# A mixture of experts on one core: the router product by token, the down matrices by column halves, and the first gather chunk by chunk

## The reference

```python
def expert_choice_moe(h, w_router, w_gate_e, w_up_e, w_down_e):
    b, s, _ = h.shape
    cap = EC_CAPACITY * s // N_EXPERTS                       # 64 tokens for each of 16 experts
    affinity = jax.nn.softmax((h @ w_router).astype(jnp.float32), axis=-1)
    top_aff, idx = lax.top_k(jnp.swapaxes(affinity, 1, 2), cap)
    bidx = jnp.arange(b)[:, None, None]
    xe = h[bidx, idx]
    hid = jax.nn.silu(jnp.einsum('becd,edf->becf', xe, w_gate_e)) * jnp.einsum('becd,edf->becf', xe, w_up_e)
    ye = jnp.einsum('becf,efd->becd', hid, w_down_e)
    return jnp.zeros_like(h).at[bidx, idx].add(ye * top_aff[..., None].astype(ye.dtype))

# in second_block, for each of the two layers i
x = x + expert_choice_moe(rms_norm(x, g_moe[i]), w_router[i], w_exp_gate[i], w_exp_up[i], w_exp_down[i])
```

## Time and profile before

| | |
|---|---|
| median of 3 runs | 3707.64 us (3706.45 to 3708.91) |
| the profiled execution: device time | 3712.06 us |
| its span | 3710.3 us |
| mean granted TensorE clock | 0.964 of full |
| TensorE matmul busy | 3504.9 us (94%) |
| weight loads busy | 2375.7 us (64%) |
| VectorE (DVE) busy | 1728.1 us (47%) |
| ScalarE (ACT) busy | 1142.2 us (31%) |
| bytes moved | 618.76 MB, mean 167 GB/s |

### The profile page before, as it was taken

The page is one execution under the profiler, slowest core; times in us unless marked ns, Lnnn a source line. Parts: engine busy times, 40 slices in busy tenths (PEclk is TensorE's granted clock), DMA queues, the critical chain, the costliest instruction groups (busy, mean ns, idle before and its releaser), DMA issues. The chain is left out here.

```text
span 3710.3 us, 44635 instructions
## 1 busy us (share of the span) xinstructions
PE 3504.9 (94%) x16784; PEld 2375.7 (64%) x16784; DVE 1728.1 (47%) x2908; ACT 1142.2 (31%) x1792; POOL 41.5 (1%) x20
## 2 busy tenths in 40 slices
PE   8899999979999999989998999999988997999997
PEld 6678877855788886747875434437746885444336
DVE  6665545378665538565334111137656334111116
ACT  5632223147422224365322000013355322000003
POOL 0000000022000000000000000000000000000000
PEclk9999999989999999989998999999989998999998
DMA  4223323120133231211225999971211324999991
GB/s 151 88 91 96 96 91 96 51 93 2 69 96 96 96 96 50 87 41 66 94 84 229 414 422 422 422 322 60 86 60 40 99 71 171 400 421 422 422 400 57
DMA packets 113080, 618.76 MB, mean 167 GB/s; under 512 B 12780, under 2 KB 13300, under 8 KB 63544
## 3 DMA queue, kind: packets, MB, share of 16 engines
q1 hardware_dynamic: 112952, 617.04, 44.0%
HBM read 614.81 MB, written 4.28 MB: 167 GB/s over the span
## 5 line engine op out<-in xcount | busy, mean ns | idle before, releaser
L398 PE MATMUL PS<-WK_r,RING_r 128*128 128x512 f32 x1920 | 749.6, 390 | 0.0
L396 PE MATMUL PS<-WK_r 128*128 128x512 f32 x1448 | 566.3, 391 | 0.0
L398 PEld LDWEIGHTS PS<-WK_r,RING_r 128*128 128x128 f32 x1920 | 360.3, 188 | 77.7
L390 ACT ACTIVATE WK_r<-RING 128x1024 fp32r<-128x1024 f32 x212 | 223.4, 1054 | 450.3 <-PE PS L398 369.8
L397 PE MATMUL PS<-HT_r,WK_r 128*128 128x512 f32 (+1 forms) x896 | 349.5, 390 | 0.0
L393 DVE TENSOR_TENSOR RING_r<-RING,WK_r 128x1024 fp32r<-128x1024 f32 x212 | 259.1, 1222 | 185.2 <-ACT WK_r L390 185.1
L396 PEld LDWEIGHTS PS<-WK_r 128*128 128x128 f32 x1448 | 271.7, 188 | 57.4 <-issue 0.5
L397 PE MATMUL PS<-HT_r,RING_r 128*128 128x512 f32 (+1 forms) x752 | 295.9, 393 | 0.0
L2479 PE MATMUL PS<-AR,WK 128*64 128x512 f32 x1152 | 264.0, 598 | 0.0
L398 PE MATMUL PS<-AR_r,RING_r 128*128 128x512 f32 x672 | 262.6, 391 | 0.0
L393 DVE TENSOR_TENSOR RING_r<-RING,RING_r 128x1280 fp32r<-128x1280 f32 (+2 forms) x96 | 132.5, 1381 | 274.2 <-ACT RING_r L390 274.2
(11 more groups left out here) (450 smaller groups left out, 5296.0 us busy)
## 6 DMA issues: line engine op xcount, KB each, us to landing
AR<-moe SPq DMA_DIRECT2D x192, 1024.0 KB, 13.4
RING<-moe SPq DMA_DIRECT2D x160, 1024.0 KB, 13.6
RING<-ff_in SPq DMA_DIRECT2D x96, 512.0 KB, 3.5
RING<-branch SPq DMA_DIRECT2D x64, 640.0 KB, 3.9
WK<-moe SPq DMA_DIRECT2D x32, 1024.0 KB, 13.9
RING<-ff_out SPq DMA_DIRECT2D x48, 512.0 KB, 3.5
RING<-mix_in SPq DMA_DIRECT2D x44, 512.0 KB, 3.6
RING<-ple SPq DMA_DIRECT2D x16, 640.0 KB, 5.4
```

What stands on the lines that cost most here:

```text
L390: return nc.scalar.activation(r(out), x, ACT.Copy)
L396: nc.tensor.matmul(out, r(w_high), r(x_high), start=start, stop=False)
L398: return nc.tensor.matmul(out, r(w_low), r(x_high), start=False, stop=stop)
```

## The change

Three things are changed in both layers.

1. `route`: the router's weights are loaded in the stage before (`load_router`, issued by SP in `out_stage` behind the prefetch of its weights). The product is turned round: the tokens of `HT` are the stationary operand and the 16 columns of `WR` move, 4 token tiles for each of the 8 chunks, which writes the logits with tokens on partitions at once. ACT's copy and the transposes of L2355 go. DVE adds the squares in pairs only, and TensorE sums the four pairs (4 by 4 matmuls with one moving column). ACT loads the root's table ahead of its wait for the mean.
2. `experts`, down matrices: the data of the 8 pieces are laid out anew by the host, so that the first four hold the left 512 output columns of all eight chunks and the last four the right ones (`down_step`). ACT and DVE take each half when its four steps are done. In the last pair the back steps 0 to 3 stand behind the down steps 4 to 7, and the back steps 4 to 7 write banks 0 to 3 without a wait for DVE's adds.
3. `experts`, first pair: `first_tokens(k)` gathers one chunk; two stand ahead of the first matrix step, and one behind each of the steps 0 to 5. ACT copies chunk by chunk.

```diff
+    router_in = whole.enter_context(nc.semaphore("router_in"))
+    WR = SM[:, 128:128 + KD * EXPERTS]
+    def load_router(l):
+        return lambda sp: sp.dma_start(WR, io["router"][l]).then_inc(router_in, 16)
...
             def _(sp):
-                sp.dma_start(WR, io["router"][l]).then_inc(s["w_in"], 16)
                 for j in range(MOE_R):
...
             def _(pe):
-                pe.wait_ge(s["w_in"], 16)
+                pe.wait_ge(router_in, 16 * (l + 1))
                 for k in range(KD):
                     pe.wait_ge(s["scaled"], k + 1)
-                    mm = nc.tensor.matmul(bank(0)[0:EXPERTS], WR[:, k * EXPERTS:(k + 1) * EXPERTS], HT[:, k],
-                                          start=(k == 0), stop=(k == KD - 1))
+                    for t in range(TT):
+                        mm = nc.tensor.matmul(bank(1, t * EXPERTS, EXPERTS), HT[:, k, t * P:(t + 1) * P],
+                                              WR[:, k * EXPERTS:(k + 1) * EXPERTS], start=(k == 0 and t == 0),
+                                              stop=(k == KD - 1), skip_group_check=True)
                 mm.then_inc(s["logits_in"], 1)
-                pe.wait_ge(s["paired"], 6)
-                for t in range(TT):
-                    for k in (0, 4):
-                        mm = nc.tensor.matmul(bank(7, t, 1), SQ[k][:, t * P:(t + 1) * P], cst("ones", 0, 1),
-                                              start=(k == 0), stop=(k == 4))
+                for n in range(KD // 2):
+                    pe.wait_ge(s["paired"], n + 1)
+                    for t in range(TT):
+                        mm = nc.tensor.matmul(bank(7, t, 1), SQ[2 * n][:, t * P:(t + 1) * P], cst("ones", 0, 1),
+                                              start=(n == 0 and t == 0), stop=(n == KD // 2 - 1), skip_group_check=True)
                 mm.then_inc(s["summed"], 1)
-                pe.wait_ge(s["logits_out"], 1)
-                for t in range(TT):
-                    mm = nc.tensor.transpose(bank(1, t * EXPERTS, EXPERTS), LT[:, t * P:(t + 1) * P],
-                                             cst("ident")[0:EXPERTS, 0:EXPERTS])
-                mm.then_inc(s["logits_t"], 1)
...
-                act.wait_ge(s["logits_in"], 1)
-                nc.scalar.activation(LT, bank(0)[0:EXPERTS], ACT.Copy).then_inc(s["logits_out"], 1)
+                nc.scalar.preload_act_table(ACT.Sqrt)
...
+                def down_step(i, n):
+                    q = 2 * KD + n
+                    pe.wait_ge(moe_filled[q % MOE_R], before + i * (16 * UN // MOE_R) + 16 * (q // MOE_R + 1))
+                    w = moe_slot(q)
+                    half = n // 4
+                    for row in range(2):
+                        k = 2 * (n % 4) + row
+                        for e in range(2):
+                            mm = nc.tensor.matmul(bank(4 + half)[e * CAP:(e + 1) * CAP], HI[:, k, e * CAP:(e + 1) * CAP],
+                                                  w[:, (2 * row + e) * TOK:(2 * row + e + 1) * TOK],
+                                                  start=(k == 0), stop=(k == KD - 1))
+                    mm.then_inc(s["used"], 1)
...
-                    if k >= 2:
+                    b = k - 4 if final and k >= 4 else 6 + k % 2
+                    if k >= 2 and b >= 6:
                         pe.wait_ge(s["added"], i * KD + (k - 1))
...
-                    for k in range(KD):
-                        matrix_step(i, 2 * KD, 4, HI, k)
-                        if k == 1:
+                    for n in range(KD):
+                        down_step(i, n)
+                        if n == 1:
                             select(parity)
+                        if final and n >= 4:
+                            back_step(i, n - 4, True)
...
-                for k in range(KD):
-                    back_step(PAIRS - 1, k)
+                for k in range(4, KD):
+                    back_step(PAIRS - 1, k, True)
...
-                    act.wait_ge(s["used"], i * UN + UN)
                     act.wait_ge(s["sel_out"], i * 3 + 3)
-                    nc.scalar.activation(r(YH), PS[:, 4:6], ACT.Copy, scale=VALUE).then_inc(s["y_high"], 1)
+                    for half in range(2):
+                        act.wait_ge(s["used"], i * UN + (2 * KD + 4 + 4 * half))
+                        nc.scalar.activation(r(YH[:, half]), bank(4 + half), ACT.Copy, scale=VALUE).then_inc(s["y_high"], 1)
...
-                y_low(PAIRS - 1)
-                add_back(PAIRS - 1)
+                y_low(PAIRS - 1, (0,))
+                add_back(PAIRS - 1, range(4))
+                y_low(PAIRS - 1, (1,))
+                add_back(PAIRS - 1, range(4, KD), True)
```

More of the change, by code:

```diff
@@ L2320, in route @@
     def route(l, pw):
-        WR = SM[:, 128:128 + KD * EXPERTS]
         AF = AFID[:, :, 1:EXPERTS + 1]
@@ L2324, in route @@
         SQ = [wk(k) for k in range(KD)]
-        LT, AT, PL = (wk(16 + n)[0:EXPERTS] for n in range(3))
+        AT, PL = (wk(17 + n)[0:EXPERTS] for n in range(2))
         VALS = wk(19)[0:EXPERTS, 0:CAP]
         logits = lambda: bank(1, 0, TT * EXPERTS).rearrange("p (t e) -> p t e", t=TT)
-        with stage("w_in scaled squared paired logits_in logits_out logits_t summed mean root act_exp aff_ready aff_t tok_t tok_out "
+        with stage("scaled squared paired logits_in summed mean root act_exp aff_ready aff_t tok_t tok_out "
                    "picked places_t hots dve_step") as (block, s):
@@ L2399, in _ @@
                     v.tensor_scalar(HT[:, k], XT[:, k], par("moe_g", l * KD + k), None, ALU.mult).then_inc(s["scaled"], 1)
-                defer_sums(dve, s, SQ)
+                for k in range(0, KD, 2):
+                    dve.wait_ge(s["squared"], k + 2)
+                    v.tensor_tensor(SQ[k], SQ[k], SQ[k + 1], ALU.add).then_inc(s["paired"], 1)
                 dve.wait_ge(s["summed"], 1)
                 v.tensor_scalar(R4, bank(7, 0, TT), 1.0 / D, EPS, ALU.mult, ALU.add).then_inc(s["mean"], 1)
-                dve.wait_ge(s["logits_t"], 1)
+                dve.wait_ge(s["logits_in"], 1)
                 step(v.tensor_reduce(MX, logits(), X, ALU.max, negate=True))
@@ L2462, in token_step, with first_tokens @@
                         mm.then_inc(s["x_in"], 1)
[L2464 to L2469, removed]
+                def first_tokens(k):
+                    for t in range(TT):
+                        mm = nc.tensor.matmul(bank(4 + k % 4, k // 4 * P, P), HN[:, t, k * P:(k + 1) * P],
+                                              HOTS[0][:, t], start=(t == 0), stop=(t == TT - 1))
                     mm.then_inc(s["first_in"], 1)
@@ L2504, in pair @@
                     if first:
-                        for n in range(2):
-                            first_tokens(n)
+                        first_tokens(0)
+                        first_tokens(1)
                     else:
@@ L2509, in pair @@
                     for k in range(KD):
-                        if first and k % 2 == 0:
-                            pe.wait_ge(s["first_out"], k // 2 + 1)
+                        if first:
+                            pe.wait_ge(s["first_out"], k + 1)
                         matrix_step(i, 0, 0, XE[parity], k)
-                        if first and k in (1, 3):
-                            first_tokens(2 + k // 2)
+                        if first and k + 2 < KD:
+                            first_tokens(k + 2)
                         if not first and k >= 2:
@@ L2564, in pair @@
                         taken(i + 1, 1 - parity)
-                    act.wait_ge(s["used"], i * UN + UN)
                     act.wait_ge(s["sel_out"], i * 3 + 3)
-                    nc.scalar.activation(r(YH), PS[:, 4:6], ACT.Copy, scale=VALUE).then_inc(s["y_high"], 1)
[L2569 to L2572, removed]
+                    for half in range(2):
+                        act.wait_ge(s["used"], i * UN + (2 * KD + 4 + 4 * half))
+                        nc.scalar.activation(r(YH[:, half]), bank(4 + half), ACT.Copy, scale=VALUE).then_inc(s["y_high"], 1)
+                for k in range(KD):
+                    act.wait_ge(s["first_in"], k + 1)
+                    nc.scalar.activation(XE[0][:, k], bank(4 + k % 4, k // 4 * P, P), ACT.Copy).then_inc(s["first_out"], 1)
                 pair(0, 0)
@@ L2581, in _, with y_low, add_back @@
                 v = nc.vector
-                def y_low(i):
-                    dve.wait_ge(s["y_high"], i + 1)
-                    for half in range(2):
+                def y_low(i, halves=(0, 1)):
+                    for half in halves:
+                        dve.wait_ge(s["y_high"], i * 2 + (half + 1))
                         v.scalar_tensor_tensor(r(YL[:, half]), bank(4 + half), VALUE, r(YH[:, half]).bitcast(F32), ALU.mult,
                                                ALU.subtract).then_inc(s["y_low"], 1)
-                def add_back(i):
-                    for k in range(KD):
+                def add_back(i, ks=range(KD), spread=False):
```

(7 more changed lines are left out.)

9 lines of the change are left out of this document (4 added, 5 removed).

## The result

| | before | after |
|---|---|---|
| median of 7 runs each | 3707.64 us | 3721.99 us (3719.25 to 3725.17) |
| ratio, 95% interval | | 1.0037 (1.0027 to 1.0047) |
| profiled execution; its span | 3712.06; 3710.3 us | 3722.43; 3720.7 us |
| mean granted TensorE clock | 0.964 | 0.962 |
| TensorE matmuls busy | 3504.9 us | 3518.2 us |

The account below looks back on a forecast made before the run. TensorE was taken to set the pace in the experts' loop, and route to be a chain. Terms 14.0 + 2.6 - 2.4 = +14.2 us, set on the 3707.64 us median, gave 3721.8 us, 0.38% slower; range 3713 to 3729.

Parts of the forecast that it names:

- Part 1, route: Route: load wait removed, but 96 narrow records mostly at half clock; +14.0 us for two layers, bounds +10.8 to +17.2.
- The wait's end: Route: TensorE starts its product at about 1974.45 instead of 1975.77, no longer waiting for the router's weights.
- the 17 records at the full clock: Route: 17 records at 0.115 us fit before the clock falls at 1976.43; the other 79 take 0.215 each.
- the 7.0 forecast: Route: the mean starts at 1993.4 instead of 1986.42, +7.0 us a layer.
- bounds of 5.4 to 8.6: Route, mean's delay a layer: +5.4 with full clock for twice as long, +8.6 with low clock from the start.
- Rival 1: Route: the clock comes back in the new product as in the old; +1.0 us a layer, total 3709.8; chance 0.15.
- A gain of 1.3 us: Route: what removing TensorE's wait for the load of the router's weights saves in a layer.
- Rival 3: Whole kernel faster: needs 7.4 us, while the load's wait and the tail give at most 5.8; chance 0.03.
- Part 2, gather: Experts' first pair: four more gather places at 0.33 us, +1.3 us a layer; two layers +2.6, bounds 0 to +8.6.
- rival 2: First gather keeps the clock low longer and the tail gains little: +19.0 us, 3726.6; chance 0.10.
- Part 3, the tail: Down matrices and last pair's end: -1.2 us a layer; two layers -2.4, bounds -3.2 to -1.0.
- smaller gain: End of experts: if the adds keep the old pace of 0.92 us, they end at 2490.5, a gain of 0.5.

Follow-up runs that it names:

- e_route: The kernel before with only the route changes (load ahead, product by token, four pair sums): 3720.62 us, ratio 1.004.
- e_wide: The whole change, but each matmul of the product by token moves 128 columns instead of 16: 3700.09 us, ratio 0.9981.
- e_load: The kernel before with only the router's weights loaded a stage ahead, product as before: 3697.19 us, ratio 0.9974.
- e_gather: The kernel before with only the first gather made chunk by chunk: 3709.92 us, ratio 1.0006.
- e_halves: The kernel before with down matrices by halves, but the last pair's eight back steps in a row behind the last down step: 3705.86 us, ratio 0.9992.
- e_down: The kernel before with only down matrices by halves and the last pair's back steps among the down steps: 3703.92 us, ratio 0.9995.
- e_best: The kernel before with the router's load ahead, down halves and interleaved last back steps; old product and gather: 3696.64 us, ratio 0.997.

## Why the prediction was right, and where its sum was off

**Part 1, route: right, in size and mechanism.** The wait's end, the 17 records at the full clock, the fall within 0.1 us of 1976.43 and the low clock until the transposes came as written. The mean moved by 7.2 and 6.9 us for the 7.0 forecast (starts at 19.66 and 19.35 us for 19.4), and e_route alone gives 13.1 of the 14.0 us. Hitting the point so closely was partly luck: in the six layers with the narrow product the fall came 1.1 to 2.75 us behind the first scaling, and in e_route the mean is 8.25 and 7.34 us later, inside the bounds of 5.4 to 8.6.

Rival 1, that a 16-column record counts as work, fell: after runs 79 of the 96 records of layer 0 without a break at 0.50. e_wide shows that the clock makes the price: its 96 records end at 11.5 us. The Trainium skill ("TensorE: Matmul & The Clock Gate", Part 1) says that activity releases the throttle. Read as busy time, the trace does not bear it out: TensorE counts as busy for 17.14 of 17.18 us and stays at 0.50. The Trainium skill's weight load of 128 columns in 107 ns (the same page, Part 2, LDWEIGHTS) lies near e_wide's pace of 0.113 us at the full clock. At half clock the sums of after go at 0.218 us, so there the trace disagrees.

**The load ahead was undervalued.** "A gain of 1.3 us" priced it against the narrow product, where the clock falls either way. It did no harm to the forecast, since the change has that product. In the old product the same load is worth 2.85 us a layer, 1.1 where the prediction looked (the wait) and 1.7 beside it (the clock behind the wait). The rest of e_load's 10.3 us lies further down: in the traces the stretch from the first scaling to the last gate activation is 3.65 and 3.2 us shorter in all, and the tail 2.6, as it holds no low stretch. Rival 3's bound, 5.8 us at most from the load and the tail, left these low stretches out: the load alone gave 10.3 us. In this change, with the narrow product, the bound was not put to the test.

**Part 2, gather: right.** From the mean to the last gate activation after is 1.2 and 1.5 us longer than before (460.02 and 460.34 against 458.84 and 458.86), for 1.3; e_gather's median is 2.4 us up for 2.6, and its trace shows 1.35 and 0.9. The clock at the start stayed low as long as before (13.7 us in both), so rival 2 did not come in this change.

**Part 3, the tail: mis-sized.** "I take -1.2 us": in the profiles the tail went from 45.8 to 42.3, -3.5. The term left out the clock: the last pair of before holds two low stretches, and after has none. The first runs from 2464.5 to 2468.0, at the first down steps, the second from 2485.0 to 2488.4, among the adds:

```profile
2465.00:2470.00 5.00, 5.00 (x18) 1.30 (x14) 0.00 (x0) 0.00 (x0) 0.00 (x0) 0.71 1.02 403
...
2485.00:2488.40 3.40, 3.38 (x8) 2.06 (x8) 2.05 (x4) 0.00 (x0) 0.00 (x0) 0.50 0.00 0
```

The prediction let the last down step start 2.4 us later than before; it starts 0.8 us later (35.0 against 34.2 us behind the gate activation), since the first stretch with its 1.6 us is gone. The second made the adds' pace of 0.92 us, from which the prediction took its smaller gain. Where TensorE holds the clock, as in e_load, the adds of the old tail go at 0.77 us:

```profile
2478.62 1.28 DVE L2597 TENSOR_TENSOR XT<-XT,PS 128x512 f32<-128x512 f32 x2 [0.22 <-PE PS L2498]
...
2483.23 1.28 DVE L2597 TENSOR_TENSOR XT<-XT,PS 128x512 f32<-128x512 f32 x2 [0.23 <-PE PS L2498]
```

(2483.23 - 2478.62) / 6 = 0.77. There part 3 is worth 43.17 - 42.30 = 0.9 us a layer, against e_gather with one low stretch 1.85, against the profile of before with two 3.5: every kernel with the whole of part 3 has a tail of 42.3, and those with the old one 43.2 to 45.8. Its own share is 0.9 us, below the 1.2 taken; 2.6 us are low stretches that before had and after had not. That part 3 avoids them is not shown: e_load avoids both without it, and e_halves, which differs from e_down only behind the fifth down step, has the first, which begins 0.1 us ahead of the first down step.

**The sum.** In the profiles the layers give 8.4 - 3.5 = +4.9 us each, 9.8 in all, and the executions differ by 10.4. The medians differ by 14.4. The profiled execution of before lay 4.4 us above its median, and part of its slow tail may have been that execution's own; with a gain of 0.9 us the sum would be 2 x (8.4 - 0.9) = 15.0. That was not shown, as only profiled executions have a trace. So the total was hit closer than its terms deserve: part 1 and part 2 were right, part 3 was off by 2.3 us a layer in the profiles, and that the medians lie within 0.2 us of the forecast is luck.

## What to carry to other kernels

A TensorE that is busy without a break can be at half clock: before a product is turned so that few columns move against full weight loads, look in the trace for the granted clock under such records, and price them at both levels. Where the narrow form is wanted, more moving columns of the same data can be free or better: here eightfold columns took 22 us off, some 17 of them in the changed layers. The old product with its load ahead still gives the mean sooner, at 9.6 against 11.5 us. And a short wait ahead of a product costs more than its length where the clock falls behind it: 1.1 us of wait cost 2.85 us a layer here. Remove the wait alone first (e_load, 10.3 us faster), before changing the product that it delays. Last, compare a stage between two profiles only after looking for low stretches in both.

## What the runs showed of the hardware that was not expected

- 64 records of 128 stationary columns take 12.18 us with 16 moving columns and 7.38 us with 128; the first ran at 0.50 from its 18th record on, the second at 1.00.
- Behind the wide product, 32 one-column records kept 1.00 for 3.63 us, while behind the narrow one they had 0.50; widening them too changed nothing (3699.98 against 3700.09 us).
- With 1.69 us of idle time ahead of it the 512-column product kept the clock, with 2.82 us it lost it. e_best speaks for the idle time and against the moment at which it came: its stage starts within 0.1 us of before's (1974.07 and 1974.00), the idle time is 1.69 us, and it has 1.00 throughout its product, also where before had 0.50:

```profile
1974.40:1981.30 6.90, 6.60 (x16) 1.48 (x16) 6.63 (x14) 3.92 (x8) 0.00 (x0) 1.00 0.90 343
```

- The idle time does not decide alone: the 16-column product lost the clock with 1.69 us ahead of it too.
- Low stretches come and go in stages that a change does not touch: the old tail of experts took 43.2, 44.1 and 45.8 us in four kernels with none, one and two of them. What decides it was not shown.
